# The entry into each wide projection: weight splits one unit earlier, PSUM waits gathered ahead of the matmuls

## The reference, cut to what matters

```
h = modulate(rms_norm(x, norm[l]), shift, scale)    # x * g / rms * (1 + scale) + shift
y = h @ w_in[l]                                     # all 512 tokens, 1024 -> many columns
x = x + gate * (...)                                # closes the block
```

## Time and profile before

| | |
|---|---|
| median of 3 runs | 2680.7 us |
| the profiled execution's own time | 2682.72 us |
| its span | 2680.7 us |
| busy: PE / DVE / ACT | 96% / 65% / 37% |
| mean granted TensorE clock | 0.992 |

### The profile page before, as it was taken

The page is one execution under the profiler, slowest core; times in us unless marked ns, Lnnn a source line. Parts: engine busy times, 40 slices in busy tenths (PEclk is TensorE's granted clock), DMA queues, the critical chain, the costliest instruction groups (busy, mean ns, idle before and its releaser), DMA issues.

```text
span 2680.7 us, 34456 instructions
## 1 busy us (share of the span) xinstructions
PE 2581.8 (96%) x11354; PEld 2050.9 (77%) x11354; DVE 1730.4 (65%) x2481; ACT 1003.7 (37%) x1525; POOL 72.9 (3%) x146
## 2 busy tenths in 40 slices
PE   4899999999999999999999999999999999999998
PEld 2688888777777787888878888877777678788886
DVE  3655577899998666543355556779999866643433
ACT  2422222555554433222232222245555443423222
POOL 0000010000000000000000000100000000000000
PEclk9999999999999999999999999999999999999998
DMA  6455466222222343543335555622222233233332
GB/s 224 122 155 156 142 198 201 81 79 80 81 74 83 94 125 111 156 125 93 99 89 157 154 155 178 219 83 83 78 75 85 75 94 90 83 97 99 92 96 94
DMA packets 469949, 311.91 MB, mean 116 GB/s; under 512 B 11047, under 2 KB 447529, under 8 KB 468872
## 3 DMA queue, kind: packets, MB, share of 16 engines
q1 hardware_dynamic: 445260, 227.69, 28.9%
q0 software_dynamic: 19584, 75.51, 8.4%
q10 hardware_dynamic: 5052, 8.02, 1.0%
HBM read 306.13 MB, written 5.05 MB: 116 GB/s over the span
## 4 chain that ended last, share of the span: by engine, by line
PE 69%; DVE 16%; issue 9%; ACT 4%; ACTq 1%; DVEq 1%
PE bank L1139 21%; PE bank L1141 21%; PE bank L1140 21%; DVE conv_part L944 6%; DVE rstd L654 3%; DVE w_lo L643 1%; DVE scaled L665 1%; ACTq L435 1%; ACT w_hi L383 1%; PE bank L1165 1%; DVE h_lo L674 1%; ACT probs L534 1%; PE bank L1160 1%; PE bank L1211 1%; ACT probs L541 1%
## 5 line engine op out<-in xcount | busy, mean ns | idle before, releaser
L643 DVE TENSOR_TENSOR w_lo<-w_raw,w_hi 128x1024 fp32r<-128x1024 f32 (+1 forms) x434 | 522.2, 1204 | 629.8 <-ACT w_hi L383 629.8
L1139 PE MATMUL bank<-h_hi,w_hi 128*128 128x512 f32 x2112 | 849.9, 402 | 14.9 <-DVE scaled L848 7.5
L1141 PE MATMUL bank<-h_hi,w_lo 128*128 128x512 f32 x2112 | 827.3, 392 | 0.0
L1140 PE MATMUL bank<-h_lo,w_hi 128*128 128x512 f32 x2112 | 825.9, 391 | 0.0
L383 ACT ACTIVATE w_hi<-w_raw 128x1024 fp32r<-128x1024 f32 (+1 forms) x434 | 451.4, 1040 | 877.5 <-PE bank L1141 875.6
L1139 PEld LDWEIGHTS bank<-h_hi,w_hi 128*128 128x128 f32 x2112 | 398.6, 189 | 124.7 <-issue 43.9
L1141 PEld LDWEIGHTS bank<-h_hi,w_lo 128*128 128x128 f32 x2112 | 398.6, 189 | 85.7
L1140 PEld LDWEIGHTS bank<-h_lo,w_hi 128*128 128x128 f32 x2112 | 399.4, 189 | 82.0 <-issue 3.8
L944 DVE SCALAR_TENSOR_TENSOR conv_part<-glu,conv_taps,conv_part 128x512 f32<-128x512 f32 x464 | 317.6, 745 | 0.0
L1139 PE MATMUL bank<-s_hi,w_hi 128*128 128x512 f32 x704 | 274.6, 390 | 0.0
L1141 PE MATMUL bank<-s_hi,w_lo 128*128 128x512 f32 x704 | 274.0, 389 | 0.0
(11 more groups left out here) (178 smaller groups left out, 2646.7 us busy)
## 6 DMA issues: line engine op xcount, KB each, us to landing
w_raw<-in_ffn_w_in SPq DMA_DIRECT2D x176, 512.0 KB, 3.9
ada_raw<-in_ada_w POOLq DMA_DIRECT2D x128, 512.0 KB, 4.8
w_raw<-in_w_mix_in SPq DMA_DIRECT2D x112, 512.0 KB, 3.7
w_raw<-in_ffn_w_out SPq DMA_DIRECT2D x64, 512.0 KB, 3.6
w_raw<-in_ffn_w_out SPq DMA_DIRECT2D x32, 384.0 KB, 3.1
w_raw<-in_w_mix_out SPq DMA_DIRECT2D x18, 512.0 KB, 3.6
ada_first<-in_ada_w POOLq DMA_DIRECT2D x8, 1024.0 KB, 24.6
w_raw<-in_w_attn_branch SPq DMA_DIRECT2D x16, 512.0 KB, 3.6
```

The costliest lines, as they stand in the source:

```text
L643: dve.tensor_tensor(wlo[slot][:, 0:n, :], raw[slot][:, 0:n, :], whi[slot][:, 0:n, :].bitcast(F32), ALU.subtract).then_inc(w_lo[slot], 1)
L1139: pe.matmul(acc, wh, hi[:, k0 + k, :], start=first and k == 0, stop=False)
L1140: pe.matmul(acc, wh, lo[:, k0 + k, :], start=False, stop=False)
L1141: mm = pe.matmul(acc, wl, hi[:, k0 + k, :], start=False, stop=last and k == n - 1)
```

## The change

Three things are edited.

1. The split of the second pair's weights moves one tile earlier, on ACT and on DVE: after tiles 1 and 3, where it was after tiles 2 and 4.
2. On DVE the reads of the banks are tied to the same table and come right behind the `w_lo` of their slot. Read 0 moves from after tile 2 to after tile 1, read 1 stays after tile 3.
3. On PE the waits for `acc_read` leave the inside of `two_slabs` (slot 0 at its step 0, slot 1 at its own step 0, four steps later). `entry` now waits for both banks ahead of each pair.

```diff
 LN_MEAN, LN_VAR = 2, 4
-SPLIT_AFTER = (2, 4)
-READ_AFTER = (2, 3)
+SPLIT_AFTER = (1, 3)
...
-                if j - 1 in READ_AFTER:
-                    t = READ_AFTER.index(j - 1)
+                if j - 1 in SPLIT_AFTER:
+                    t = SPLIT_AFTER.index(j - 1)
+                    w_lo_part(pair + 1, t)
                     dve.wait_ge(w_used[t], pair + 1)
                     dve.tensor_tensor((F[1], SQ)[t][:, :], G[t][:, :], RSTD[:, :], ALU.mult).then_inc(acc_read[t], 1)
-                if j - 1 in SPLIT_AFTER:
-                    w_lo_part(pair + 1, SPLIT_AFTER.index(j - 1))
...
-        def two_slabs(pair, use, ready, shift=None, at={}):
+        def two_slabs(pair, ready, shift=None, at={}):
...
                         pe.wait_ge(w_hi[slot], pair + 1)
                         pe.wait_ge(w_lo[slot], pair + 1)
-                        pe.wait_ge(acc_read[slot], use)
...
         def entry(l, k, name):
             n = l * 3 + k
-            pair, use = l * PAIRS + PAIR0[name], l * USES + USE0[name]
+            for t in range(2):
+                pe.wait_ge(acc_read[t], l * USES + USE0[name])
             pe.wait_ge(sem("shift_parts"), 2 * (n + 1))
-            two_slabs(pair, use, lambda j: pe.wait_ge(sem("plain_lo"), n * KT + j + 1), k,
+            two_slabs(l * PAIRS + PAIR0[name], lambda j: pe.wait_ge(sem("plain_lo"), n * KT + j + 1), k,
                       {3: lambda: norm_mean(l * AUXN + AUX_NORM[k], (n + 1) * KT if n else KT)})
-            two_slabs(pair + 1, use + 1, lambda j: pe.wait_ge(sem("unit_lo"), l * UNITS + UNIT_NORM[k] + j + 1))
+            for t in range(2):
+                pe.wait_ge(acc_read[t], l * USES + USE0[name] + 1)
+            two_slabs(l * PAIRS + PAIR0[name] + 1, lambda j: pe.wait_ge(sem("unit_lo"), l * UNITS + UNIT_NORM[k] + j + 1))
```

## The result

| | us |
|---|---|
| before, median of 4 runs | 2681.7 (2678.3 to 2683.0) |
| changed, median of 4 runs | 2700.25 (2699.1 to 2701.9) |
| ratio | 1.0073, 95% interval 1.0059 to 1.0085 |
| forecast | 2700.6, range 2690 to 2708 |

The account below looks back on a forecast made before the run. PE, busy nearly all the time, was taken to bound the kernel. Later starts of 14.9 us and 5.0 us of clock made 19.9 us on a median of 2680.7, so 2700.6 us, range 2690 to 2708.

Parts of the forecast that it names:

- The gathered wait at the second pair: PE, second pair of each entry: held until read 1 ends, behind an extra w_lo; 6.6, 1.7 and 6.6 us.
- The sum of the waits: Later starts on PE over all six entries: 6.6 + 1.7 + 6.6 = 14.9 us.
- The first gathered wait: PE, first pair: 1.43 us late in the fourth entry, 0.28 us in mixing entries, already inside the 14.9 us.
- The earlier split by itself: ACT and DVE: the early w_hi frees nothing, costs 1.5 us of DVE idle time; its benefit is lost.
- The clock: PE: six falls to half clock behind the new 4 us gaps, for three at the first tile, +5.0 us.
- the clock costs nothing extra: Rival, 0.27: falls only change places, or PE starts at full clock after a gap; 2695.6 or 2690.6 us.
- Longer falls: Rival, 0.12: 5.9 us at half clock instead of 3.4 before the second pair, 1.3 us each; 2710 us.
- Taken back downstream: Rival, 0.05: mixing heads or feed-forward tiles have slack against PE and absorb the delay; 2689 us.

Follow-up runs that it names:

- second_inside: The changed kernel with only the wait ahead of the second pair put back inside two_slabs: 2692.25 us, ratio 1.0044.
- read_first: The changed kernel with each bank's read ahead of the w_lo of its slot on DVE: 2685.7 us, ratio 1.0015.
- fill_pairs: The changed kernel with 14 small unused fp32 matmuls ahead of the gathered wait for the second pair: 2691.0 us, ratio 1.0034.
- fill_tile: The kernel before with 6 small unused fp32 matmuls between a feed-forward entry's pairs and the first tile: 2677.1 us, ratio 0.9981.
- fill_first_inside: The changed kernel with 14 small unused matmuls ahead of the second pair's wait and the first pair's wait back inside: 2687.1 us, ratio 1.0020.
- order_only: The changed order on ACT and DVE alone, with both waits of PE back inside: 2684.7 us, ratio 1.0016.
- waits_only: The kernel before with only the two gathered waits of PE added: 2679.4 us, ratio 0.9991.
- first_inside: The changed kernel with only the wait ahead of the first pair put back inside two_slabs: 2699.6 us, ratio 1.0072.
- late_read: The changed kernel with read 1 one tile later on DVE, after tile 4 in place of tile 3: 2711.4 us, ratio 1.0111.

## Why the prediction was right

**The gathered wait at the second pair** was named as the main cost, with read 1 behind the extra `w_lo` as what makes it late. Both are borne out: with this wait back inside 8.0 us come back (second_inside), and with the reads ahead of `w_lo` 14.5 us (read_first), although that kernel keeps the earlier split and both waits. It is 3.5 us above the kernel before. For the fourth entry the times are measured against the last matmul of the block before it, in the changed kernel and in the kernel before:

```profile
1379.30 0.39 PE L1139 MATMUL bank<-s_hi,w_lo 128*128 128x512 f32 x1
1371.53 0.39 PE L1141 MATMUL bank<-s_hi,w_lo 128*128 128x512 f32 x1
```

They end at 1379.69 and 1371.92, so 7.76 us are taken off (from the unrounded times). The links of the chain are:

| | forecast | measured |
|---|---|---|
| `w_hi` 0 starts | 1385.47 | 1385.34 |
| read 1 starts | 1392.16 | 1392.08 |
| second pair starts | 1393.1 | 1392.87 |
| slot 0 done, with the clock's 1.7 us | 1403.3 | 1402.83 |
| next tile, with the clock's 1.7 us | 1406.5 | 1406.03 |

**The sum of the waits** was 14.9 us. With the clock kept up on both sides it is 2691.0 - 2677.1 = 13.9 us (fill_pairs against fill_tile). That is the cleanest single test of this term. Entry by entry, from the end of the block before to the next tile or the scores, the two profiles differ by 1.8 to 2.0 us in a feed-forward entry (forecast 2.2) and by 3.1 us in a mixing one (forecast 3.3).

**The first gathered wait** was forecast inside that sum, as 1.43 us of later start in three entries and 0.28 in two, 4.9 us together. PE's first matmul came 1.4 us late in the fourth entry, and the wait costs 3.9 us in all (fill_first_inside).

**The earlier split by itself** was said to free nothing and to leave DVE idle. Alone it costs 3.7 us (order_only). I was too short on it: it is not only an order that gains nothing but one of the two things that make the loss. Gathered waits with the old order cost 1.4 to 2.3 us with the clock taken out (waits_only), because read 1 then stands ahead of `w_lo` 1 and behind no idle time. Most of the loss needs both.

**The clock** was forecast as six falls for three, 10.0 us against 5.0. Measured were 2700.25 - 2691.0 = 9.3 us for the changed kernel and 2682.2 - 2677.1 = 5.1 us for the kernel before. The waits and the clock together give 13.9 + 9.3 - 5.1 = 18.1 us. This sum is no test: it is 2700.25 - 2682.2 by construction, and differs from the measured 18.5 only by the kernel before, 2682.2 on that chip and 2681.7 beside the changed kernel. A test is the changed kernel's profile, where PE worked at half clock for 21.4 us at the entries. Half of that is 10.7 us, against 9.3 by filling. The rival *the clock costs nothing extra* (0.27) falls with this. *Longer falls* (0.12) came true in one entry of six. That it stayed at one was partly luck: in first_inside, with the same gaps, five of six falls were long, and nothing in the working told the two apart. *Taken back downstream* falls. The scores stand 6.0 us late in the second entry, and after all mixing heads the tile behind the gap starts at 841.09, still 6.0 us late:

```profile
841.09 0.77 PE L1137 MATMUL bank<-h_hi,w_hi 128*128 128x512 f32 x1 [3.44 <-DVE w_lo L642]
```

**What the steps had wrong** is small. PE follows read 1 by 0.1 us (1400.52 to 1400.63) in place of 0.25, which is 0.9 us over six entries. The other 0.5 us between 19.9 forecast and 18.5 measured is less than the runs scatter, and I don't assign it. The reading that the clock falls each time behind a gap of 3.46 us, taken from two cases, does not hold in general: over all profiles it fell behind 19 of 26 such gaps (last section).

## What to carry to other kernels

A wait that is gathered from the middle of a software pipeline to its head holds up work that did not need it. What that costs depends on the order of the engine that releases it: here some 2 us with read 1 ahead of the weight split, and some 15 us (order_only to the changed kernel, the clock's extra falls included) with it behind. An instruction moved earlier on an engine that works in order has to be checked for what it waits for, since everything queued behind it waits too. Price the clock apart from the waits, by filling the idle time with work that nobody needs; otherwise a run can hide a real saving, as first_inside did, or a real cost, as waits_only did.

## What the runs showed of the hardware

Whether the clock fell after an idle gap of PE, counted over the profiles:

| idle gap | where | falls |
|---|---|---|
| 1.2 to 1.7 us | waits_only, second pair of each entry and first tile | 0 of 10 |
| 1.7 us | read_first, first tile of the first and sixth entries | 0 of 2 |
| 1.9 us | before, first tile | 3 of 4 |
| 2.2 us | read_first, second pair | 4 of 6 |
| 2.5 us | second_inside and order_only, first tile | 6 of 8 |
| 3.4 to 3.5 us | all 13 profiles, at about 835 and 2130 us, outside the entries | 19 of 26 |
| 3.9 to 4.0 us | after and first_inside, second pair | 12 of 12 |
| 5.3 us | late_read, second pair | 6 of 6, five of them for 6.8 us |

The length of the gap alone does not decide. In second_inside the clock stayed at 1.00 behind both gaps of 3.44 us. Here is the first, and the window behind it:

```profile
836.93 0.47 PE L1137 MATMUL bank<-h_hi,w_hi 128*128 128x512 f32 x1 [3.44 <-DVE w_lo L642]
...
836.93:840.30 3.37, 3.37 (x15) 2.78 (x16) 3.37 (x6) 0.00 (x0) 0.00 (x0) 1.00 0.53 155
```

What decides, no run here shows.

I had not expected that small fp32 matmuls of constants are enough to hold the clock: 14 of them in 3.29 us of a 3.9 us gap did, and 6 in 1.50 us of a 1.9 us gap did. Nor had I expected the length of a low stretch to differ between profiles of nearly the same gap, with 3.4 us in the changed kernel and 6.8 us in first_inside for 3.93 us idle in the fourth entry. It goes with the kernel and not with the single execution: the mean granted clock is 0.990 or 0.991 in all 13 executions of the changed kernel on record, and 0.987 or 0.988 in all five of first_inside.
